# Causal masks of two attentions added by fp32r products of an fp32r identity and fp32r tables

## The reference, cut to what matters

```python
# forgetting attention: query block q0:q1 against keys 0:q1
logits = einsum(q[:, q0:q1], k[:, :q1]) * scale + c[q0:q1, None] - c[None, :q1]
logits = where(kpos <= qpos, logits, -inf)
out = softmax(logits) @ v[:, :q1]

# stick-breaking attention: the same blocks
z = einsum(q[:, q0:q1], k[:, :q1]) * scale
mask = kpos < qpos
log_one_minus = where(mask, log_sigmoid(-z), 0)
suffix = cumsum(log_one_minus, reverse) - log_one_minus
w = where(mask, exp(log_sigmoid(z) + suffix), 0)
out = w @ v[:, :q1]
```

## Time and profile before

| | us |
|---|---|
| median of 3 runs | 2983.03 |
| the runs | 2982.72, 2983.03, 2989.16 |
| span of the profiled execution | 2987.6 |
| busy: TensorE, its loads | 2913.4, 2434.3 |
| busy: VectorE, ScalarE, GpSimd | 961.7, 744.5, 1642.4 |

### The profile page before, as it was taken

The page is one execution under the profiler, slowest core; times in us unless marked ns, Lnnn a source line. Parts: engine busy times, 40 slices in busy tenths (PEclk is TensorE's granted clock), DMA queues, the critical chain, the costliest instruction groups (busy, mean ns, idle before and its releaser), DMA issues.

```text
span 2987.6 us, 35633 instructions
## 1 busy us (share of the span) xinstructions
PE 2913.4 (98%) x14824; PEld 2434.3 (81%) x14824; DVE 961.7 (32%) x1447; ACT 744.5 (25%) x1492; POOL 1642.4 (55%) x1338
## 2 busy tenths in 40 slices
PE   8989999999999999999999999999999999999998
PEld 7777888888888768888888888788888887888887
DVE  3845404211025484141110333732110238521102
ACT  2236323101024373231100222542000233420001
POOL 4840472666657604726666467526666566166663
PEclk9999999999999999999999999999999998999999
DMA  4331331333223204213322332013222231132222
GB/s 141 99 127 57 114 126 57 99 99 99 99 85 120 71 15 141 99 57 113 99 94 92 105 99 95 5 39 113 92 97 99 99 106 57 35 113 94 99 99 85
DMA packets 184548, 271.21 MB, mean 91 GB/s; under 512 B 6708, under 2 KB 145972, under 8 KB 184388
## 3 DMA queue, kind: packets, MB, share of 16 engines
q1 hardware_dynamic: 174240, 243.28, 24.5%
q10 hardware_dynamic: 10148, 25.66, 2.6%
HBM read 266.79 MB, written 2.13 MB: 90 GB/s over the span
## 4 chain that ended last, share of the span: by engine, by line
PE 81%; DVE 8%; DMA 4%; POOL 3%; ACT 2%; issue 1%; ACTq 0%; DVEq 0%; POOLq 0%
PE PS L485 24%; PE PS L486 23%; PE PS L487 23%; POOL wlo L2395 3%; PE PS L877 3%; PE PS L574 2%; DVE a_qk L1303 2%; PE PS L863 1%; DVE nmx L1638 1%; PE PS L1031 1%; ACT whi L634 1%; DMA raw<-mem_wkv 1%; PE PS L1489 1%; DMA raw<-ffn_w 1%; DVE s_c L2283 0%
## 5 line engine op out<-in xcount | busy, mean ns | idle before, releaser
L2395 POOL TENSOR_TENSOR wlo<-raw,whi 128x512 fp32r<-128x512 f32 x881 | 1169.8, 1360 | 543.4 <-ACT whi L634 543.4
L485 PE MATMUL PS<-xT_hi,whi 128*128 128x512 f32 (+1 forms) x2304 | 848.0, 368 | 12.7 <-DVE xT_lo L594 6.4
L486 PE MATMUL PS<-xT_lo,whi 128*128 128x512 f32 (+1 forms) x2304 | 843.7, 366 | 0.0
L487 PE MATMUL PS<-xT_hi,wlo 128*128 128x512 f32 (+1 forms) x2304 | 843.5, 366 | 0.0
L2387 POOL TENSOR_SCALAR whi<-raw 128x1024 fp32r<-128x1024 f32 x384 | 416.6, 1103 | 666.0 <-DMA raw<-ffn_w 226.0
L485 PEld LDWEIGHTS PS<-xT_hi,whi 128*128 128x128 f32 x2304 | 435.9, 189 | 88.5 <-DVE xT_lo L594 8.7
L486 PEld LDWEIGHTS PS<-xT_lo,whi 128*128 128x128 f32 x2304 | 435.9, 189 | 70.4 <-issue 1.0
L487 PEld LDWEIGHTS PS<-xT_hi,wlo 128*128 128x128 f32 x2304 | 435.8, 189 | 70.3
L1073 DVE TENSOR_TENSOR htmp<-sil,PS 128x512 f32<-128x512 f32 x88 | 56.5, 683 | 803.4 <-ACT sil L1058 803.4
L485 PE MATMUL PS<-whi,h_hi 128*128 128x512 f32 x704 | 274.8, 390 | 0.8 <-POOL wlo L2395 0.8
L487 PE MATMUL PS<-whi,h_lo 128*128 128x512 f32 x704 | 274.0, 389 | 0.0
(11 more groups left out here) (384 smaller groups left out, 3142.8 us busy)
## 6 DMA issues: line engine op xcount, KB each, us to landing
raw<-ffn_w SPq DMA_DIRECT2D x66, 1024.0 KB, 5.1
raw<-ffn_w_gu SPq DMA_DIRECT2D x44, 1024.0 KB, 5.1
raw<-ffn_w_down SPq DMA_DIRECT2D x22, 1024.0 KB, 4.9
raw<-mem_wkv SPq DMA_DIRECT2D x16, 1024.0 KB, 5.3
raw<-even_w_in SPq DMA_DIRECT2D x14, 1024.0 KB, 5.1
raw<-ev_w_in SPq DMA_DIRECT2D x14, 1024.0 KB, 5.2
raw<-odd_w_in SPq DMA_DIRECT2D x12, 1024.0 KB, 5.2
raw<-od_w_in SPq DMA_DIRECT2D x10, 1024.0 KB, 5.1
```

The costliest lines, as they stand in the source:

```text
L485: pe.matmul(o, lhs[0], rhs[0], start=start, stop=False, skip_group_check=True)
L486: pe.matmul(o, lhs[0], rhs[1], start=False, stop=False, skip_group_check=True)
L487: return pe.matmul(o, lhs[1], rhs[0], start=False, stop=stop, skip_group_check=True)
L2395: m = pool.tensor_tensor(wlo[b][:, cs], raw[b][:, cs], whi[b][:, cs].bitcast(F32), ALU.subtract)
```

## The change

A tile of four fp32r tables of 128 columns is added. ScalarE copies the first 512 columns of par into it, right behind the second panel's cut at the start. TensorE waits for this once ahead of each of the two attentions, and the mask products take the fp32r identity and the fp32r table.

```diff
+        masks = small("masks", [P, 4, 128], F32R)
...
+        ident_r, le_r, lt_r = (masks[:, i, :] for i in (0, 2, 3))
...
+        masks_ready = sem("masks_ready")
...
-                    return [pe.matmul(PS[:, b, chunk(t)], ident, pcol("le"), start=False, stop=True, skip_group_check=True)
+                    return [pe.matmul(PS[:, b, chunk(t)], ident_r, le_r, start=False, stop=True, skip_group_check=True)
                             for b in (other, bank)]
...
+                pe.wait_ge(masks_ready, 1)
                 pe_units(pe, A, scores, values, lambda u: (exp_done, A.u0 + u + 1))
...
-                    return [pe.matmul(PS[:, b, chunk(t)], ident, pcol("lt"), start=False, stop=True, skip_group_check=True)
+                    return [pe.matmul(PS[:, b, chunk(t)], ident_r, lt_r, start=False, stop=True, skip_group_check=True)
                             for b in (other, bank)]
...
+                pe.wait_ge(masks_ready, 1)
                 pe_units(pe, A, scores, values, lambda u: (G["sb_weights"], u + 1))
...
             act_cut(act, 1)
+            act.wait_ge(par_loaded, 16)
+            act.activation(masks[:, :, :].rearrange("p a b -> p (a b)"), par[:, 0:512], ACT.Copy).then_inc(masks_ready, 1)
             code[0]["head"]["act"](act, lambda: [act_turn(act, xT_hi, 0, KD, 2 * t, t) for t in (2, 3)])
```

## The result

| | before | after |
|---|---|---|
| median, 20 runs each, in turn on the same chip (us) | 2985.28 | 3002.26 |
| lowest and highest run | 2980.95, 2998.02 | 2985.93, 3017.42 |
| profiled execution: span, mean granted clock | 2987.6, 0.993 | 3009.0, 0.979 |

The kernel after is slower: ratio 1.0054, 95% interval 1.0040 to 1.0068. I had forecast 2978.7 us, with a range of 2975 to 2985; the time is outside the range, on the side to which I gave 0.08. Its runs spread over 31 us and go with their mean granted clock: the shortest, 2985.93 us, had 0.991, the longest, 3017.42, had 0.978. The profiled execution, at 0.979, is one of the long ones: 21.4 us above the span of before, where the medians lie 17.0 us apart.

What follows compares the result with a forecast made beforehand. TensorE, busy 98% of the span, was taken as the bound, except early in each attention. Savings of 2.6 (forgetting) + 1.8 (stick-breaking) - 0.1 (waits) = 4.3 us, from the median 2983.03, gave 2978.7 us; range 2975 to 2985.

Steps and rivals of the forecast that it cites:

- the side to which I gave 0.08: Whole kernel: slower by over 0.2% (about 6.0 us), through the late clock rise and scatter; chance 0.08.
- rival (c): Stick-breaking attention: TensorE's clock rises later, 4 us later costing 2 us (2980.7); chance 0.08 some us, 0.04 much later.
- the 2.6 and 1.8 saved: Savings in us forecast for the first stretch (forgetting attention) and the second (stick-breaking attention).
- at half clock it has no gap from there either: Stick-breaking attention from 2528 us: argument against a later clock rise, from TensorE busy 21.97 of 22 us.
- a rise over 20 us later: Stick-breaking attention: clock rising this late makes the kernel over 0.2% slower, each us of half clock costing half a us.
- The mask's own price: Both attentions: a pair's masks cost 0.33 us in place of 0.55, saving 0.22, at 0.11 us a record.
- (a): Both attentions' masks: narrow fp32r is no cheaper than fp32, so nothing is saved, 2983.1 us; chance 0.14.
- (b): Both attentions' masks: the fp32r weight load is quicker, 0.32 us saved a pair, 5.7 us in all, 2977.3; chance 0.12.
- the eleven on TensorE's own chain: Forgetting attention: eleven of 16 pairs start at 1928.8 us or later and save 0.22 us each, 2.4 together.
- VectorE's gaps: Stick-breaking attention: two idle gaps, 0.82 and 0.71 us, ahead of longer rows; to shrink below 0.1 us, saving 0.77 and 0.71.
- The other edits: ScalarE's copy at the start, some 0.6 us, hidden in idle time; TensorE's two waits, 0.1 us taken for both.
- 0.70 for no change: Whole kernel: chance 0.70 that the time stays within 0.2% (6.0 us); the forecast saving of 4.3 lies inside it.

Runs made afterwards that it cites:

- e4: Against the kernel before: each mask product is two fp32r records of 128 columns, the first adding zeros; ratio 1.0063, median 3007.49 us.
- e9: Against the kernel before: mask products of both attentions left out, so the attention isn't causal; ratio 1.0018 (0.9998-1.0037), median 2995.46 us.
- e5: Against the kernel after: masks of row block 0 in both attentions back to fp32, blocks 1 to 3 fp32r; ratio to before 1.0014, median 2991.62 us.
- e7: Against the kernel after: masks of row blocks 0 to 2 back to fp32, only block 3 fp32r; ratio to before 1.0003, median 2987.57 us.
- e10: Against before: fp32r masks in row blocks 2 and 3, unread 512-column products at stick-breaking's barrier and in its first six pairs; ratio 0.9977, median 2983.32 us.
- e12: Against before: fp32 masks kept, unread 512-column products added at stick-breaking's barrier and in its first six pairs; ratio 0.9993 (0.9983-1.0003), median 2984.36 us.
- e3: Against the kernel before: each mask product is two fp32r records of 256 columns, padded with zeros; ratio 1.0002, median 2988.62 us.

## Why the prediction was wrong

**The step that failed is rival (c), the clock.** I had priced it as the fall's length in one stretch only, the second, put the clock's cost in the first at nothing, and gave it 0.12 in all, 0.04 for the size that came. In the profile the first stretch lost 15.2 us by it and the second 13.0, in place of the 2.6 and 1.8 saved. Two arguments stood against it. The first: "at half clock it has no gap from there either, as it had none when the clock rose", which takes it that TensorE without a gap raises the clock and keeps it. The earlier trace rows only showed that this went together once. After the change TensorE was busy 44.00 of 44 us at 0.50, and e4 77.00 of 77. The Trainium skill ("TensorE: Matmul & The Clock Gate", section Why this matters for your kernels) advises to keep TensorE continuously busy, without idle gaps between matmuls, so that it stays at its full clock; the rows here don't bear that out as enough, and the measurement decides. The second: that the first stretch had 1.00 in both windows of the earlier trace rows. That was read as safe; it only said that it had not fallen yet. In e9's profile the clock fell there with less work and in e4's with as many records and loads, so it stood near an edge that no row of before showed.

**Where the rise would come.** I wrote that a rise over 20 us later makes the kernel slower by more than 0.2%, at half a us for each us. In the profiled execution the clock was 0.50 up to 2571 and 1.00 from 2572 on, some 53 us after the stretch's start, where before had some 19: 34 us later. At my own price that is 17 us, less the 1.8 saved some 15; the stretch lost 13.0. So the price was near; what I had wrong was that the clock would rise because TensorE has no gap.

**What a half clock costs a pair.** The chain of waits in the kernel after, one pair at half clock, and the three pieces of a pair at full clock.

```profile
1931.38 1.16 PE PS L2146 x4
1932.54 0.62 PE PS L2152 x2
1933.15 0.45 PE PS L867 x2
...
1935.52 1.58 PE PS L2146 x4
```

```profile
1965.19 1.06 PE PS L2146 x4
1966.25 0.37 PE PS L2152 x2
1966.62 0.46 PE PS L867 x4
```

The masks' piece of the chain is 0.37 us in place of 0.64: the saving that I predicted, somewhat more. At half clock the pair takes 4.14 us (1931.38 to 1935.52) instead of 2.6: it loses 1.5 us to save 0.27.

**The mask's own price was right to 0.05 us.** The loads and the next line's matmul, as in the earlier trace rows:

```profile
1966.18 0.30 PEld L2152 LDWEIGHTS PS<-masks 128*128 128x128 f32 x2 [0.76 <-issue]
1966.42 0.42 PEld L867 LDWEIGHTS PS<-par,f_p 128*128 128x128 f32 x4
...
1966.46 0.63 PE L867 MATMUL PS<-par,f_p 128*128 128x128 f32 x4
```

The next line's load comes 0.24 us after the first mask's (I said 0.22; 0.44 would have been (a), 0.12 (b)), its matmul 0.28 us after it, where I had 0.33 and before had 0.55. Two loads of 0.12 us are the whole price; so a pair saves 0.27 us where I took 0.22. Rival (a), that narrow fp32r is no cheaper, and rival (b), that its load is quicker, are both out. The stretches at full clock in e5 to e7 agree with 0.22 to 0.25 us a pair. e5's 2.68 us, for 12 of the 16 pairs, are near the 2.4 that I gave the eleven on TensorE's own chain; the first four pairs stayed fp32 there, so the 2.6 for the whole stretch was never seen by itself.

**The second stretch.** The 1.8 us never came into sight: no kernel with one narrow record for every mask kept the clock. VectorE's gaps, which I said would fall below 0.1 us, grew:

```profile
2550.22 0.96 DVE L2288 TENSOR_TENSOR_SCAN s_c<-s_neg,s_zero 128x384 f32<-128x384 f32 x1 [2.46 <-ACT s_neg L2235]
...
2572.22 1.23 DVE L2288 TENSOR_TENSOR_SCAN s_c<-s_neg,s_zero 128x512 f32<-128x512 f32 x1 [3.12 <-ACT s_neg L2235]
```

2.46 and 3.12 us in place of 0.82 and 0.71: at half clock the scores come later than VectorE asks for them. In e10, at full clock and with half of the masks in fp32r, they are 0.57 and 0.16. In e12, with the same unread products and fp32 masks, they are before's:

```profile
2531.93 0.96 DVE L2292 TENSOR_TENSOR_SCAN s_c<-s_neg,s_zero 128x384 f32<-128x384 f32 x1 [0.82 <-ACT s_neg L2239]
...
2545.01 1.23 DVE L2292 TENSOR_TENSOR_SCAN s_c<-s_neg,s_zero 128x512 f32<-128x512 f32 x1 [0.70 <-ACT s_neg L2239]
```

So the masks, not the clock, took 0.25 and 0.54 us out of the gaps, 0.79 together, and e10's stretch is 0.77 shorter than e12's: the mechanism of the second stretch is shown. Whether both gaps would close with all masks changed stays open.

**The other edits.** They cost nothing, as predicted. The copy, and ScalarE's idle time behind it, in the kernel after:

```profile
19.21 0.61 ACT L2419 ACTIVATE masks<-par 128x512 fp32r<-128x512 f32 x1
...
29.41 1.09 ACT L586 ACTIVATE xT_hi<-PS 128x512 fp32r<-128x512 f32 x2 [9.58 <-PE PS L578]
```

0.61 us (I said 0.6), with 9.58 us of idle time left of the earlier trace rows. The two waits don't show: e3 has them and is at 1.0002. That the gain of the stretches passes through to the end is borne out by the loss, which did: the spans differ by what the stretches and the start do, within 0.9 us.

**The chances.** 0.70 for no change rested on the mask's price, which I had well, and on the clock, which I had from two windows of one execution. The spread of the runs was a sign that I passed over: of the three shown before, one was 6.4 us above the others, and I took it as scatter without a cause. In the runs here such differences go with the mean clock. The range, 2975 to 2985, was drawn from (b) to (a) and left (c) out. And (b), 5.7 us, lay inside the 6.0 us of no change, so most of its chance belonged there and not to "faster".

## What to carry to other kernels

Before you take cheap records out of a stretch of small matmuls, or make them cheaper, ask what they do for TensorE's clock: the profile's busy share doesn't tell, the row of the granted clock does, and a product whose price is its weight load passes few columns for its time. Price the whole stretch at half clock as a case of its own; here 0.27 us a pair stood against 1.5. If the saving is wanted, take it where the units are wide, hold the clock elsewhere with wide unread products in TensorE's waiting time, and time it in a dozen runs, since the clock differs between executions of one kernel. Compare the clocks of these runs as well as their times.

## What the runs showed of the hardware

- TensorE can be shown busy without a gap at 1.2 GHz (a granted clock of 0.50) for long: 44.00 of 44 us in the kernel after, with 20 records in 4 us instead of 31.
- At equal records, loads and waits, 256 moving columns a record kept the clock at 1.00 (49.38 us), 128 lost it (0.58, 77.00 us). That columns through the array are what counts is the reading that fits all of the runs, e9's too; no run measured how much of them is wanted, and the theory has no number.
- An fp32r product of 128 columns with 128 columns of weights takes 0.12 us at full clock (0.24 for two), as one of 256 columns does; that its weight load sets this is the reading that fits, also for e4, where four such records of a pair start 0.11 us apart at full clock and 0.21 us at half.
- Less work made both stretches longer (e9: 51.26 for 48.96 us and 61.82 for 59.14, one execution each), and unread work made one shorter (e12: 58.64 for 59.14).
- The granted clock of a stretch isn't a property of the kernel alone. The same kernel after took 2985.93 us at a mean of 0.991 and 3017.42 at 0.978. What makes the one or the other of two executions stays open.
